# One product for both heads of a pair in each level of the RWKV inverse

## The chip, the cores and the metric

One core of a Trainium2 chip runs the whole program. The metric is the device time of one execution in microseconds, median of three runs: 1650.59 us before the change (1650.26 to 1653.68).

## The reference

Two layers of a diffusion backbone over 256 context tokens and 256 latent tokens of width 1024. Each layer mixes tokens in four parallel branches, merges them by gates, and ends in a convolutional feed-forward block. Branch D is a bidirectional RWKV-7 recurrence with four heads of 64 dimensions:

```
def step(s, inp):
    r_t, w_t, k_t, v_t, kk_t, a_t = inp
    sa = jnp.einsum('bhvk,bhk->bhv', s, kk_t)
    s = (s * w_t[:, :, None, :] - sa[..., None] * (kk_t * a_t)[:, :, None, :]
         + v_t[..., None] * k_t[:, :, None, :])
    return s, (jnp.einsum('bhvk,bhk->bhv', s, r_t) if emit else None)
```

It runs over context and then latent tokens, once forward and once backward. All is in float32.

## The kernel before

The kernel does the recurrence in eight chunks of 64 tokens. Within a chunk the effect of all `sa` terms on each other is the inverse of a 64x64 unit triangular matrix, for each head. The inverse `TN` is built by doubling: it is right for blocks of 2 tokens, and each level z of 2, 4, 8, 16, 32 joins two neighbouring blocks of z into one of 2z.

Layout: the 128 partitions hold two chunks (x = 0, 1; tokens of chunk 2b + x in half x), b runs over the four blocks of 128 tokens, p over the two pairs of heads, y over the heads of a pair. TensorE's 128x128 array is used in corners: an operand in partition half x and an output in partition half y take one 64x64 corner.

One pass is one direction of one layer, so there are four. In TensorE's program (the block of `pe`) a pass has, in this order: the masked token products (L2607, L2619), bonus and token-major copies (L2625, L2596), the five levels, u0 (L2696), `at` (L2704), the chunk recurrence (L2720 to L2736, with parts of the modulation, L2428 and L2436, between), the read-out products (L2746, L2758, L2762). A level has:

- sx (L2645), for each p: the level's triangular factor `LM1` times the even blocks of `TN`. The stationary operand is one head's 64x64 block of LM1, the moving one its 32 even columns. 16 products for each p.
- tt (L2633): `TN` of both heads turned by four 128x128 transposes for each p, copied to `TT` by ScalarE (L1322).
- jobs put between (`LEVEL_EXTRA`): LM2's products in levels 2 and 4, turned keys and `ta` in level 8, `xv` and turned betas in levels 16 and 32; in the forward passes also parts of the backward pass's preparation.
- sy (L2685), for each p: `TT` (64x64, one head and chunk) times the masked sx (`XS`), 32 columns. 16 products for each p.

VectorE masks each sx to `XS` (L1970, 256 elements a partition) and subtracts each sy from the even blocks of TN (L1987). Next level's sx waits for that subtraction. Each engine runs its program in order; the order is written by hand in one job list, and results go to PSUM banks that are handed out in that order. Weights of 1 MB stream through a ring of three slots by SP's queue; ScalarE and VectorE split them into high and low parts (L1065, L1610).

Of the kernel before, what the change touches and what calls it, by code (L numbers as in the profile page):

```python
# [74 lines left out]
for _n, _c in VEC_COLS:  # L75
# [7 lines left out]
              ("m2", CH2), ("m4", CH2), ("m8", CH2), ("m16", CH2), ("m32", CH2), ("eye", CH), ("cos", LAT), ("sin", LAT),  # L83
# [31 lines left out]
def constants():  # L115
# [303 lines left out]
def build(nc, a, out):  # L419
    ctx = ExitStack()  # L420
    with ctx:
# [283 lines left out]
        def even_blocks(v, z):  # L705

            if len(v.shape) == 2:
                return v.rearrange("p (g two n) -> p g two n", two=2, n=z)[:, :, 0, :]
            return v.rearrange("p b y (g two n) -> p b y g two n", two=2, n=z)[:, :, :, :, 0, :]
# [883 lines left out]
        def _(dve):  # L1593
# [136 lines left out]
            for l in range(LAYERS):  # L1730
# [205 lines left out]
                for d in range(2):  # L1936
                    it = 2 * l + d

                    def masked(name, LM, p):
                        h = slice(2 * p, 2 * p + 2)  # L1940
                        s = filled(dve, (name, l, d, p)).rearrange("p y (b n) -> p y b n", b=NB)
                        if l:
                            dve.tensor_tensor(LM[:, h, 0:2, 0:CH], s[:, :, 0:2, 0:CH],
                                              K("lm", CH).unsqueeze(1).unsqueeze(1).to_broadcast([P, 2, 2, CH]), ALU.mult)
                        b0 = 2 * l
                        dve.tensor_tensor(LM[:, h, b0:, :], s[:, :, b0:, :],
                                          K("lm", 2 * CH).unsqueeze(1).unsqueeze(1).to_broadcast([P, 2, NB - b0, 2 * CH]),
                                          ALU.mult).then_inc(frees((name, l, d, p)), 1)

                    def half_mask(name):  # L1950
                        return K(name, CH2).unsqueeze(1).unsqueeze(1).to_broadcast([P, 2, NB, CH2])
# [338 lines left out]
        def _(pe):  # L2290
# [201 lines left out]
            for l in range(LAYERS):  # L2492
# [97 lines left out]
                for d in range(2):  # L2590
# [7 lines left out]

                    def corners():
# [36 lines left out]
                    for n, z in enumerate(LEVELS):  # L2636
                        for p in range(2):
# [13 lines left out]
                        for extra in LEVEL_EXTRA(l, d, n):  # L2651
# [19 lines left out]
                            elif extra[0] == "xv":  # L2671
# [3 lines left out]
                                for b, x, y in corners():  # L2675
                                    h = 2 * p + y
                                    last = pe.matmul(o[side(y), x, CH * b:CH * b + CH], LM2[side(x), h, b, 0:CH],
                                                     tokm["v"][side(x), b, HD * h:HD * h + HD], start=True, stop=True)
                                done(last)
                        for p in range(2):  # L2680
# [69 lines left out]
                    for p in range(2):  # L2750
                        o = job(("y23", l, d, p))
                        for c in range(NCH // 2 * l, NCH):
# [3 lines left out]
                            for y in range(2):  # L2756
                                h = 2 * p + y
                                pe.matmul(o[side(y), x, dst], tokm["v"][side(x), b, HD * h:HD * h + HD],  # L2758
                                          LM2[side(x), h, b, CH:2 * CH], start=True, stop=False)
                            for y in range(2):  # L2760
                                h = 2 * p + y
# [140 lines left out]
```

## Time and profile before

| | |
|---|---|
| median of three runs | 1650.59 us |
| profiled execution | 1652.26 us, its span 1650.2 us |
| TensorE matmul, busy | 1586.6 us, 96% |
| TensorE weight loads, busy | 1321.7 us, 80% |
| VectorE / ScalarE / GpSimd, busy | 944.0 / 799.6 / 312.5 us |
| mean granted TensorE clock | 0.990 |

### The profile page before, as it was taken

The page shows a single profiled execution, that of the slowest core. Times are in us where ns is not written, and L with a number is a line of the kernel's source. Part 1 is how long each engine was busy: PE and PEld are TensorE (multiplying, and loading weights), DVE is VectorE, ACT ScalarE, POOL GpSimd, SP SyncE. Part 2 cuts the span into 40 slices and gives each one's busy share as a digit, 9 for nine tenths or more (in the row PEclk, how much of TensorE's full clock was granted, in tenths as well). Part 3 has the DMA queues.
Part 4 walks back from the last instruction along what each step waited for, and adds up shares of the span by engine and source line. Part 5 has one row for each costly group of instructions (what it writes and reads, how often), then busy time and mean ns, then how long its engine had stood idle before and what let it go on. Part 6 is the DMA issues. An engine that isn't in the chain of part 4 may idle for free.

```text
span 1650.2 us, 33271 instructions
## 1 busy us (share of the span) xinstructions
PE 1586.6 (96%) x14140; PEld 1321.7 (80%) x14140; DVE 944.0 (57%) x1497; ACT 799.6 (48%) x1315; POOL 312.5 (19%) x251
## 2 busy tenths in 40 slices
PE   8999999988899999999999999999998889999998
PEld 6788767767678887888888886987877779899987
DVE  5364555565465569655554225655776277677764
ACT  4322456473354266443443225525766365566653
POOL 0160234323110000112222000312352220012210
PEclk9999999999999999999999999999999899999999
DMA  9753334223852352322226343843413285645453
GB/s 332 198 166 102 102 103 160 75 99 102 266 192 91 113 191 77 102 91 88 95 71 111 106 123 126 261 128 115 143 56 130 55 281 179 215 165 181 164 189 134
DMA packets 213889, 234.42 MB, mean 142 GB/s; under 512 B 5936, under 2 KB 194736, under 8 KB 213744
## 3 DMA queue, kind: packets, MB, share of 16 engines
q1 hardware_dynamic: 194208, 191.14, 35.3%
q0 software_dynamic: 14928, 34.87, 7.9%
q10 hardware_dynamic: 4608, 6.29, 1.1%
q8 instruction: 114, 1.87, 0.5%
q14 instruction: 31, 0.25, 0.0%
HBM read 216.55 MB, written 15.73 MB: 141 GB/s over the span
## 4 chain that ended last, share of the span: by engine, by line
PE 70%; DVE 4%; issue 3%; ACT 3%; DMA 0%; POOL 0%; ACTq 0%; DVEq 0%; POOLq 0%
PE ps L2337 15%; PE ps L2338 15%; PE ps L2339 15%; PE ps L2633 1%; PE ps L2645 1%; PE ps L2428 1%; PE ps L2794 1%; PE ps L2793 1%; PE ps L2792 1%; PE ps L2685 1%; PE ps L2402 1%; PE ps L2404 1%; PE ps L2403 1%; PE ps L2362 1%; PE ps L2363 1%
## 5 line engine op out<-in xcount | busy, mean ns | idle before, releaser
L1065 ACT ACTIVATE whi<-ring 128x1024 fp32r<-128x1024 f32 (+1 forms) x262 | 274.5, 1052 | 481.6 <-PE ps L2339 424.6
L1610 DVE TENSOR_TENSOR wlo<-ring,whi 128x1024 fp32r<-128x1024 f32 (+1 forms) x262 | 327.5, 1254 | 175.5 <-ACT whi L1065 174.8
L2337 PE MATMUL ps<-H,whi 128*128 128x256 f32 (+1 forms) x640 | 215.4, 337 | 1.8 <-DVE wlo L1610 1.8
L2339 PE MATMUL ps<-H,wlo 128*128 128x256 f32 (+1 forms) x640 | 214.9, 336 | 0.0
L2338 PE MATMUL ps<-H,whi 128*128 128x256 f32 (+1 forms) x640 | 214.9, 336 | 0.0
L2337 PE MATMUL ps<-HR,whi 128*128 128x512 f32 (+1 forms) x568 | 202.1, 356 | 0.5 <-DVE wlo L1610 0.3
L2339 PE MATMUL ps<-HR,wlo 128*128 128x512 f32 (+1 forms) x568 | 198.3, 349 | 0.0
L2338 PE MATMUL ps<-HR,whi 128*128 128x512 f32 (+1 forms) x568 | 198.2, 349 | 0.0
L2337 PEld LDWEIGHTS ps<-H,whi 128*128 128x128 f32 x640 | 122.3, 191 | 14.2 <-issue 1.9
L2338 PEld LDWEIGHTS ps<-H,whi 128*128 128x128 f32 x640 | 122.2, 191 | 12.2
L2339 PEld LDWEIGHTS ps<-H,wlo 128*128 128x128 f32 x640 | 122.3, 191 | 12.0
L2337 PEld LDWEIGHTS ps<-HR,whi 128*128 128x128 f32 x568 | 107.5, 189 | 18.1 <-issue 3.8
L2338 PEld LDWEIGHTS ps<-HR,whi 128*128 128x128 f32 x568 | 107.5, 189 | 14.0 <-issue 0.7
L2339 PEld LDWEIGHTS ps<-HR,wlo 128*128 128x128 f32 x568 | 107.4, 189 | 14.1
L956 POOL TENSOR_SCALAR pr<-pr,stat 128x512 f32<-128x512 f32 (+1 forms) x48 | 72.3, 1517 | 233.2 <-DVE stat L1908 233.2
L2337 PE MATMUL ps<-HG,whi 128*128 128x512 f32 (+1 forms) x256 | 87.5, 342 | 1.5 <-DVE YB L2051 1.0
L1021 POOL TENSOR_TENSOR CU<-CU,rs 128x512 f32<-128x512 f32 (+1 forms) x22 | 40.1, 1825 | 256.2 <-ACT rs L1547 256.2
L2339 PE MATMUL ps<-HG,wlo 128*128 128x512 f32 (+1 forms) x256 | 86.5, 338 | 0.0
L2338 PE MATMUL ps<-HG,whi 128*128 128x512 f32 (+1 forms) x256 | 86.5, 338 | 0.0
L1021 POOL TENSOR_TENSOR CU<-CU,rt 128x512 f32<-128x512 f32 (+1 forms) x22 | 39.7, 1804 | 139.0 <-ACT rt L1547 139.0
L2337 PE MATMUL ps<-UA,whi 128*128 128x512 f32 x160 | 62.2, 389 | 0.0
L2338 PE MATMUL ps<-UA,whi 128*128 128x512 f32 x160 | 62.2, 389 | 0.0
(397 smaller groups left out, 3279.9 us busy)
## 6 DMA issues: line engine op xcount, KB each, us to landing
ring<-in_ffn_up SPq DMA_DIRECT2D x44, 1024.0 KB, 5.0
ring<-in_w_gate SPq DMA_DIRECT2D x32, 1024.0 KB, 5.9
ring<-in_ada_w SPq DMA_DIRECT2D x32, 1024.0 KB, 5.3
ring<-in_w_in SPq DMA_DIRECT2D x24, 1024.0 KB, 7.6
ring<-in_ffn_down SPq DMA_DIRECT2D x10, 1024.0 KB, 5.0
ring<-in_ffn_down SPq DMA_DIRECT2D x18, 512.0 KB, 3.8
ada<-in_ada_w SPq DMA_DIRECT2D x8, 1024.0 KB, 11.7
WB<-in_w_branch POOLq DMA_DIRECT2D x8, 1024.0 KB, 6.5
```

Of the source, the lines that this page charges most:

```text
L956: pool.tensor_scalar(pr[:, u % 4, 0:nk], pr[:, u % 4, 0:nk], stat[:, 2, u % 4:u % 4 + 1], None, ALU.mult).then_inc(p_ready, 1)
L1021: pool.tensor_tensor(u, u, (rs, rt)[j % 2][:, c0:c1], ALU.mult).then_inc(u_ready, 1)
L1065: act.activation(whi[HALF_SLOT[m]][:, 0:kn, :], ring_half(raw, half, kn), ACT.Copy).then_inc(hi_done, 1)
L1610: dve.tensor_tensor(wlo[HALF_SLOT[m]][:, 0:kn, :], ring_half(raw, half, kn), whi[HALF_SLOT[m]][:, 0:kn, :].bitcast(F32), ALU.subtract).the ...
L2337: pe.matmul(o[:, c0:c1], hi[:, i, :], part(0, k), start=(k == 0), stop=False)
L2338: pe.matmul(o[:, c0:c1], hi[:, i, :], part(1, k), start=False, stop=False)
L2339: last = pe.matmul(o[:, c0:c1], lo[:, i, :], part(0, k), start=False, stop=(k == kn - 1))
L2362: pe.matmul(o, hi[:, k, :], part(0, k)[:, c0:c1], start=(k == 0), stop=False)
L2363: pe.matmul(o, hi[:, k, :], part(1, k)[:, c0:c1], start=False, stop=False)
L2402: pe.matmul(outs[b], u[0], wide(hi, x), start=(k == 0), stop=False)
L2403: pe.matmul(outs[b], u[0], wide(lo, x), start=False, stop=False)
L2404: last = pe.matmul(outs[b], u[1], wide(hi, x), start=False, stop=(k == FT - 1))
```

## The change

In each level both heads of a pair share one product.

- sx: the stationary operand is both heads' blocks of LM1 (64 rows, 128 columns), the moving one the even blocks of both heads' TN (64 columns). The output has 128 partitions and 64 columns for each chunk; where one head meets the other it holds values that nobody wants. 8 products for each p.
- The masks m2 to m32 are 64 wide and also zero those mixed blocks. `XS` doubles to 512 elements a partition.
- sy: the stationary operand is TT with all 128 rows (64 columns), the moving one XS with 128 rows and 64 columns; a zeroed half adds nothing. 8 products for each p, in one bank.
- LM1 and LM2 are laid out with the two heads side by side. The constants grow by 160 columns.

```diff
-              ("m2", CH2), ("m4", CH2), ("m8", CH2), ("m16", CH2), ("m32", CH2), ...
+              ("m2", CH), ("m4", CH), ("m8", CH), ("m16", CH), ("m32", CH), ...
@@ constants
-        put(f"m{z}", ((s // z) % 2 == 1) & (even // z == s // z - 1))
+        own = ((s // z) % 2 == 1) & (even // z == s // z - 1)
+        put(f"m{z}", np.concatenate([own & (p[:, None] // CH == y) for y in range(2)], 1))
@@ buffers
-        XS = at("XS", 88, [2, 2, NB, CH2])
+        XS = at("XS", 88, [2, 2, NB, 2 * CH2])
-        LM1 = at("LM1", 96, [HEADS, NB, 2 * CH])
-        LM2 = at("LM2", 104, [HEADS, NB, 2 * CH])
+        LM1 = at("LM1", 96, [2, NB, 2, 2, CH])
+        LM2 = at("LM2", 104, [2, NB, 2, 2, CH])
@@ VectorE, masked() (the same element counts, written p b a y n)
-                        s = filled(dve, (name, l, d, p)).rearrange("p y (b n) -> p y b n", b=NB)
+                        s = filled(dve, (name, l, d, p)).rearrange("p y (b a n) -> p y b a n", b=NB, a=2)
+                        o = LM[:, p, :, :, :, :].rearrange("p b a y n -> p y b a n")
@@ VectorE, each level
-                            s = filled(dve, ("sx", l, d, z, p))[:, :, 0:NB * CH2].rearrange("p x (b n) -> p x b n", b=NB)
-                            dve.tensor_tensor(XS[:, p, :, :, :], s, half_mask(f"m{z}"), ALU.mult)\
+                            s = filled(dve, ("sx", l, d, z, p))[:, :, 0:NB * CH].rearrange("p x (b n) -> p x b n", b=NB)
+                            dve.tensor_tensor(XS[:, p, :, :, :], s, own_head(f"m{z}"), ALU.mult)\
...
-                            s = filled(dve, ("sy", l, d, z, p))[:, :, 0:NB * CH2]                                .rearrange("p y (b g n) -> p b y g n", b=NB, n=z)
-                            t = even_blocks(TN[:, p, :, :, :], z)
+                            s = filled(dve, ("sy", l, d, z, p))[:, 0, 0:NB * CH].rearrange("p (g n) -> p g n", n=z)
+                            t = even_blocks(TN[:, p, :, :, :].rearrange("p b y n -> p (b y n)"), z)
@@ TensorE, sx
-                            for b, x, y in corners():
-                                last = pe.matmul(o[side(y), x, CH2 * b:CH2 * b + CH2].rearrange("k (g n) -> k g n", n=z),
-                                                 LM1[side(x), 2 * p + y, b, 0:CH], even_blocks(TN[side(x), p, b, y, :], z),
+                            for b, x in chunks:
+                                both = TN[side(x), p, b, :, :].rearrange("p y n -> p (y n)")
+                                last = pe.matmul(o[:, x, CH * b:CH * b + CH].rearrange("k (g n) -> k g n", n=z),
+                                                 LM1[side(x), p, b, 0, :, :].rearrange("k y n -> k (y n)"), even_blocks(both, z),
@@ TensorE, sy
-                            for b, x, y in corners():
-                                last = pe.matmul(o[side(x), y, CH2 * b:CH2 * b + CH2], TT[side(y), p, b, x, :],
-                                                 XS[side(y), p, x, b, :], start=True, stop=True)
+                            for b, x in chunks:
+                                last = pe.matmul(o[side(x), 0, CH * b:CH * b + CH], TT[:, p, b, x, :],
+                                                 XS[:, p, x, b, :], start=True, stop=True)
```

## Rows read from the trace of the kernel before

**Rows 1.** The page: engines' busy time; the chain that ended last, by engine.
```profile
PE 1586.6 (96%) x14140; PEld 1321.7 (80%) x14140; DVE 944.0 (57%) x1497; ACT 799.6 (48%) x1315; POOL 312.5 (19%) x251
PE 70%; DVE 4%; issue 3%; ACT 3%; DMA 0%; POOL 0%; ACTq 0%; DVEq 0%; POOLq 0%
```

**Rows 2.** Table of stretches: a backward pass's levels, first layer.
```profile
core 0: us, PE busy (x) PEld busy (x) DVE busy (x) ACT busy (x) POOL busy (x), PEclk, DMA share, GB/s
388.00:417.40 29.40, 25.45 (x898) 22.73 (x896) 10.68 (x23) 12.64 (x24) 9.42 (x11) 1.00 0.39 111
```

**Rows 3.** Groups by form: shapes, count, busy us, mean ns, idle before.
```profile
L2645 PEld LDWEIGHTS ps<-TN,LM 64*64 64x64 f32 x1280 | 22.6, 134 | 12.6 <-issue 11.3 <-DVE TN L1987 1.2
...
L2436 PEld LDWEIGHTS ps<-con,mrow 128*128 128x128 f32 x192 | 25.0, 190 | 9.4 <-issue 7.4
...
L2540 PEld LDWEIGHTS ps<-lora,w2a 64*128 64x128 f32 x32 | 2.4, 184 | 2.1 <-issue 2.1
...
L1970 DVE TENSOR_TENSOR XS<-ps,con 128x256 f32<-128x256 f32 x40 | 16.6, 423 | 13.5 <-PE ps L2645 13.2
...
L1963 DVE TENSOR_TENSOR TN<-ps,con 128x512 f32<-128x512 f32 x8 | 5.4, 680 | 0.0
```

**Rows 4.** Timeline (start us, us, engine, line), products in levels 2 and 4.
```profile
322.92 1.10 PE L2607 MATMUL ps<-ar,zk 64*64 64x128 f32 x32
323.85 1.08 PE L2685 MATMUL ps<-XS,TT 64*64 64x32 f32 x64
...
327.47 1.09 PE L2633 MATMUL ps<-con,TN 128*128 128x128 f32 x8
328.50 1.10 PE L2607 MATMUL ps<-ar,zk 64*64 64x128 f32 x32
...
393.00 1.14 PE L2645 MATMUL ps<-TN,LM 64*64 64x32 f32 x64 [0.82 <-issue]
```

**Rows 5.** Timeline, weight loads of four forms, each from its own stretch.
```profile
427.00 0.52 PEld L2436 LDWEIGHTS ps<-con,mrow 128*128 128x128 f32 x4
...
329.53 0.30 PEld L2540 LDWEIGHTS ps<-lora,w2a 64*128 64x128 f32 x4 [0.17 <-issue]
...
334.94 1.94 PEld L2664 LDWEIGHTS ps<-con,ar 64*64 64x64 f32 x63 [0.17 <-issue]
...
313.03 0.88 PEld L2585 LDWEIGHTS ps<-prT,E 128*64 128x64 f32 x16 [1.04 <-issue]
```

**Rows 6.** DMA issues: the later part of the constants.
```profile
con<-in_const SPq DMA_DIRECT2D x1, 944.0 KB, 11.2
```

**Rows 7.** Timeline, loads of the second pair's sx in level 2.
```profile
321.27 0.59 PEld L2645 LDWEIGHTS ps<-TN,LM 64*64 64x64 f32 x32 [0.39 <-issue]
...
1279.54 0.59 PEld L2645 LDWEIGHTS ps<-TN,LM 64*64 64x64 f32 x32 [0.69 <-issue]
```

**Rows 8.** Timeline, where TensorE resumes; idle time before in brackets.
```profile
414.01 0.20 PEld L2677 LDWEIGHTS ps<-X,LM 64*64 64x64 f32 x4 [1.43 <-issue]
...
1291.54 0.86 PEld L2633 LDWEIGHTS ps<-con,TN 128*128 128x128 f32 x8 [1.80 <-issue]
...
1304.85 0.29 PEld L2645 LDWEIGHTS ps<-TN,LM 64*64 64x64 f32 x4 [2.38 <-issue]
...
446.80 0.27 PE L2762 MATMUL ps<-LM,nu 64*64 64x64 f32 x2 [2.79 <-issue]
```

**Rows 9.** The page: DMA queue of TensorE's instructions; packets, MB, share.
```profile
q8 instruction: 114, 1.87, 0.5%
```

**Rows 10.** Timeline and stretch (PEclk third from last), last level to u0, backward passes.
```profile
411.01 0.86 PEld L2633 LDWEIGHTS ps<-con,TN 128*128 128x128 f32 x8
417.41 0.79 PEld L2696 LDWEIGHTS ps<-XV,TT 64*64 64x64 f32 x43 [0.46 <-ACT TT L1322]
...
1305.21 1.57 PEld L2633 LDWEIGHTS ps<-con,TN 128*128 128x128 f32 x8
1312.97 1.76 PEld L2696 LDWEIGHTS ps<-XV,TT 64*64 64x64 f32 x64 [0.33 <-ACT TT L1322]
...
1305.00:1313.00 8.00, 8.00 (x125) 6.76 (x124) 1.41 (x4) 2.99 (x5) 2.15 (x3) 0.50 0.28 68
```

More of the change, by code:

```diff
@@ L82 @@
 CONST_COLS = [("ones", P), ("fold", 2), ("ident", P), ("heads", P), ("swap", P), ("lm", 2 * CH), ("m1", CH),
-              ("m2", CH2), ("m4", CH2), ("m8", CH2), ("m16", CH2), ("m32", CH2), ("eye", CH), ("cos", LAT), ("sin", LAT),
+              ("m2", CH), ("m4", CH), ("m8", CH), ("m16", CH), ("m32", CH), ("eye", CH), ("cos", LAT), ("sin", LAT),
               ("reset", T), ("window", GRID_W)]
@@ L705, in even_blocks @@
         def even_blocks(v, z):
-            if len(v.shape) == 2:
-                return v.rearrange("p (g two n) -> p g two n", two=2, n=z)[:, :, 0, :]
-            return v.rearrange("p b y (g two n) -> p b y g two n", two=2, n=z)[:, :, :, :, 0, :]
+            return v.rearrange("p (g two n) -> p g two n", two=2, n=z)[:, :, 0, :]
         def done_at(name):
@@ L1939, in masked, with own_head @@
                     def masked(name, LM, p):
-                        h = slice(2 * p, 2 * p + 2)
-                        s = filled(dve, (name, l, d, p)).rearrange("p y (b n) -> p y b n", b=NB)
+                        s = filled(dve, (name, l, d, p)).rearrange("p y (b a n) -> p y b a n", b=NB, a=2)
+                        o = LM[:, p, :, :, :, :].rearrange("p b a y n -> p y b a n")
                         if l:
-                            dve.tensor_tensor(LM[:, h, 0:2, 0:CH], s[:, :, 0:2, 0:CH],
+                            dve.tensor_tensor(o[:, :, 0:2, 0, :], s[:, :, 0:2, 0, :],
                                               K("lm", CH).unsqueeze(1).unsqueeze(1).to_broadcast([P, 2, 2, CH]), ALU.mult)
                         b0 = 2 * l
-                        dve.tensor_tensor(LM[:, h, b0:, :], s[:, :, b0:, :],
-                                          K("lm", 2 * CH).unsqueeze(1).unsqueeze(1).to_broadcast([P, 2, NB - b0, 2 * CH]),
+                        mask = K("lm", 2 * CH).rearrange("p (a n) -> p a n", a=2)
+                        dve.tensor_tensor(o[:, :, b0:, :, :], s[:, :, b0:, :, :],
+                                          mask.unsqueeze(1).unsqueeze(1).to_broadcast([P, 2, NB - b0, 2, CH]),
                                           ALU.mult).then_inc(frees((name, l, d, p)), 1)
-                    def half_mask(name):
-                        return K(name, CH2).unsqueeze(1).unsqueeze(1).to_broadcast([P, 2, NB, CH2])
+                    def own_head(name):
+                        return K(name, CH).unsqueeze(1).unsqueeze(1).to_broadcast([P, 2, NB, CH])
                     def square_mask(name):
@@ L2597, in token_major @@
                         done(last)
+                    chunks = [(c // 2, c % 2) for c in range(NCH)]
                     def corners():
@@ L2676, in _ @@
                                     h = 2 * p + y
-                                    last = pe.matmul(o[side(y), x, CH * b:CH * b + CH], LM2[side(x), h, b, 0:CH],
+                                    last = pe.matmul(o[side(y), x, CH * b:CH * b + CH], LM2[side(x), p, b, 0, y, :],
                                                      tokm["v"][side(x), b, HD * h:HD * h + HD], start=True, stop=True)
@@ L2758, in _ @@
                                 pe.matmul(o[side(y), x, dst], tokm["v"][side(x), b, HD * h:HD * h + HD],
-                                          LM2[side(x), h, b, CH:2 * CH], start=True, stop=False)
+                                          LM2[side(x), p, b, 1, y, :], start=True, stop=False)
                             for y in range(2):
-                                h = 2 * p + y
                                 last = pe.matmul(o[side(y), x, dst], nu[side(x), b, y, HD * p:HD * p + HD],
-                                                 LM1[side(x), h, b, CH:2 * CH], start=False, stop=True)
+                                                 LM1[side(x), p, b, 1, y, :], start=False, stop=True)
                         done(last)
```

## The prediction

> **What bounds the kernel now.** I read the page first: TensorE is busy for 96% of the span and carries most of the chain of waits [rows 1]. So time added to TensorE's stream is added to the kernel, unless TensorE was waiting there. The change lies in the RWKV inverse: four passes (two layers, two directions) of five levels, 20 levels of a first product (sx), four-block transposes (tt), other small jobs, and a second product (sy). The table of stretches gives one such pass 29.4 us, with 898 matmul records and 896 weight loads in it [rows 2]. All four together are some 128 us.
>
> In the groups by form, what a level issues is 64 records for sx and 64 for sy. An fp32 product is two records, and 1280 records over 20 levels is 64 each [rows 3]. Yet 64 records take only 1.14 us on the timeline [rows 4], though one lasts 0.22: four 64x64 corners of the array run side by side.
>
> What times them is the load of the stationary operand. 64 loads take 1.05 us, the last of them 0.135 [rows 3], so the other 0.91 us are 15 steps of about 0.06 us for four loads at once. Two corners alone, with a moving operand of 64 columns instead of 32, keep the same step: 63 loads in 1.94 us, 31 steps, 0.058 us (the third of [rows 5]). So neither moving columns up to 64 nor the number of corners counts here, but the 64 stationary columns do.
>
> **First product.** Its 64 records become 32: two row halves side by side, 128 stationary columns, 64 moving. Two rows show loads of 128 columns. Where the moving operand is 2 wide, so that only the load can take time, four take 0.52 us, the last 0.19: 0.11 us a step (the first of [rows 5]; its mean of 190 ns in [rows 3]). In the 64*128 form, four take 0.30 us with a mean of 0.184: one further step of 0.115 us for a pair, so the halves load side by side (the second of [rows 5]; its mean in [rows 3]). New loads: 16 steps, 15 x 0.11 + 0.19 = 1.84 us; the products end about 0.1 us behind, as now (1.14 against 1.05). That is some 1.98 us against 1.14, **+0.84 us a level, +16.8 us in 20**. Bounds: 0 if a step stayed at 0.058, and +50 us if the halves loaded one after another (32 steps of 0.11, 3.6 us). I take 0.11, as both rows of 128 columns have it.
>
> **Second product.** 64 records become 32 in the 128*64 form, two column halves, 64 stationary columns, 64 moving. The same form with 128 moving columns loads 16 in 0.88 us, 0.106 us a pair (the fourth of [rows 5]); two 64*64 corners with 64 moving columns need 0.058. The load has 64 columns and the moving operand has 64, so the second is nearer: 16 steps of 0.058, as now. **0**; upper bound 16 x 0.048 = 0.77 a level, +15 us; lower bound 0, since the load's own step stays.
>
> **Changes of shape.** Between products of one shape the next begins before the last ends: sy starts at 323.85 behind LM2's products that end at 324.02 (322.92 + 1.10), 0.17 us early. Behind a change of shape it is 0.06 early (327.47 + 1.09 = 328.56, next at 328.50) [rows 4]. New changes come where the job ahead of sy is 64*64: levels 2 and 8 of the forward direction, levels 2, 4 and 8 of the backward one, 10 in all. Each costs 0.11 us; sy to sx changes shape too, but there TensorE waits for VectorE anyway. **+1.2 us** with the first load in the open; 0 to 2.
>
> **VectorE.** The mask of sx goes from 256 to 512 elements a partition, 0.42 to about 0.68 us (the row of a 512-element masked copy) [rows 3], 40 times, +10 us of VectorE time. Its cover is tt and the jobs between sx and sy, over 2 us in every level; without it 0.26 us a level would show at most, 5 us. It also sits ahead of the LM2 masks in the queue, but those wait for products issued behind tt. The subtraction stays at 256 elements. The other layout of LM1 and LM2 leaves element counts as they are, so 0. The constants grow by 80 KB on 944 [rows 6], in the weights' queue at the start: 80 of 1024 KB, by the 11.2 us to landing at most 0.9, I take **+0.1 us**.
>
> **What goes: waits.** In the first level the second pair's sx waits for VectorE's first inverse in three of the passes: 0.39 and 0.69 us [rows 7], and 0.16 between them in time. The first pair's sx now takes 0.42 us longer and covers that: 0.39 + 0.42 + 0.16, **-1.0 us**.
>
> The larger item: TensorE stops in the midst of a stream of equal products, with nothing before it but "issue", most in the backward passes: 1.43, 1.80 and 2.38 us are the longest [rows 8]. I count ten such stops in the levels, with a sum of 9.0 us (the others are 0.46, 0.79, 0.44, 0.68, 0.56, 0.16 and 0.25). The page's queue of instructions gives a reason: 114 packets, 1.87 MB, 16.4 KB each [rows 9]. TensorE's 28280 loads and matmuls over 114 packets make 248 a packet. Counting loads, products and waits in the order of the trace, the stops lie 256 instructions or a multiple apart. In the backward pass 1794 instructions in 29.4 us are a packet every 4.2 us [rows 2]; over the whole kernel it is one in 14.5. The change takes 640 instructions out of a pass, and stretches it: 1154 in about 31 us, one packet in 6.9 us. I expect all ten stops to go, **-9.0 us** (0 to -9).
>
> The Trainium skill ("Runtime: NRT & Kernel Launch", "Instruction fetch mechanics") has the same 16 KiB blocks of 256 instructions, but says their fetch is hidden by the pace of issue. By that rule the stops have another cause and stay; that is rival 2.
>
> Behind the stop of 2.38 us the granted clock is 0.50, the lower level (1.2 GHz), for the rest of that pass. From the transposes of its last level to u0 it takes 1305.21 to 1312.97, 7.76 us; the same stretch of the other backward pass at full clock takes 411.01 to 417.41, 6.40, less its stop of 1.5, 4.9 us [rows 8, 10]. The difference is 2.9 us. If the stop goes, what precedes the fall of the clock goes: **-2.9 us** (0 to -3.5, with u0 in it).
>
> **Sum.** 16.8 + 0 + 1.2 + 0.1 - 1.0 - 9.0 - 2.9 = **+5.2 us**. On the profiled execution (1652.26 us, span 1650.2) that is 1657.5. It stands 1.7 us above the median of 1650.59, and stops and clock differ from run to run, so I put the change on the median: **1655.8 us**.
>
> **Rivals.**
> 1. *The wide load costs no more than the narrow one in a stream* (0.058 a pair). Place: sx in all 20 levels. Then the sum is 5.2 - 16.8 = -11.6, **1639.0**: faster. Each 0.01 us on the step is 16 x 20 x 0.01 = 3.2 us, so it turns from slower to faster below 0.094 us. For it: no row has a long stream of 64*128. Against it: both rows of 128 columns, one of them with nothing else to time it.
> 2. *The stops stay*, being the loads of saved activations that POOL issues then, or slow fetches whatever the pace. No -9.0 and no -2.9: +17.1, **1667.7**. For it: the backward passes have those DMAs. Against it: the spacing by 256 instructions.
> 3. *The relief reaches further.* The same stops come behind the passes, 2.79 us in the read-out products of the first layer's backward pass (the last of [rows 8]) and one like it in the forward pass. Fewer instructions shift where packets end there: one of the two and one of 1.6 us in u0 gone makes 5.2 - 4.3 = +0.9, **1651.5**: the same. Against it: these bursts keep all their instructions.
> 4. *Column halves of sy don't run in step*: 0.106 a pair, +15, **1670.8**. The Trainium skill ("TensorE: Matmul & The Clock Gate", "Part 3: Packing small matmuls") says that a load overlaps running products only where the row group differs; with all 128 rows in use it would not here. The 128*64 row speaks against the worst of it: 16 loads with 128-column products would take over twice its 0.88 us if nothing ran side by side.
>
> That the change does not do what it says I give no weight: the diff halves both loops over corners.
>
> **Chances.** Forecast 0.45 (own range 1651.5 to 1660: 0.10 of it same, 0.35 slower); rival 1: 0.12; rival 2: 0.15; rival 3: 0.20 (0.12 same, 0.08 faster); rival 4: 0.08. Within 0.2% (3.3 us) is about what a measurement can't tell from no change. Faster 0.20, same 0.22, slower 0.58. The range for 8 in 10 reaches to rival 1 and rival 2: 1641 to 1669.
>
> **What would show it.** In the profile after: 640 records each for sx and sy; the 32 loads of a level's sx in about 1.84 us, those of sy in 1.05; no "issue" idle over 0.4 us within the levels of the backward passes; 104 packets in the instruction queue (2560 instructions less, 10 packets); clock 1.00 to the end of the last pass. It is wrong if sx's step is not 0.11, if sy takes over 1.2 us, or if stops of 1 us and more are still there with half as many records.

## The result, and the profile after

| | before | after |
|---|---|---|
| median, first comparison (7 runs each) | 1652.69 us | 1663.24 us |
| its spread | 1650.26 to 1654.57 | 1656.89 to 1672.27 |
| ratio, 95% interval | | 1.0072 [1.0045, 1.0098] |
| profiled execution, its span | 1652.26, 1650.2 | 1672.27, 1670.3 |

The change made the kernel slower, by some 10.5 us here and by 12.8 in a second comparison (below). 1655.8 was forecast, +5.2; slower had 0.58, and the time is in the range. By the number alone rival 2 (1667.7) is nearer than the forecast; only the traces tell the two apart. The profiled execution after is the slowest of its seven, so the 20 us between the two profiles are not the change's price; much of this part is about taking them apart.

The page of the kernel after: engines' busy time and TensorE's instruction queue, which answer to [rows 1, 9].

```profile
PE 1611.6 (96%) x12860; PEld 1341.4 (80%) x12860; DVE 955.0 (57%) x1497; ACT 799.2 (48%) x1315; POOL 313.6 (19%) x251
...
q8 instruction: 104, 1.70, 0.4%
```

The groups by form of the kernel after, for [rows 3]: shapes, count, busy us, mean ns, idle before.

```profile
L2648 PE MATMUL ps<-TN,LM 64*128 64x64 f32 x640 | 40.6, 274 | 6.1 <-issue 3.9 <-DVE TN L1987 1.1 <-DVE LM L1946 0.2
L2648 PEld LDWEIGHTS ps<-TN,LM 64*128 64x128 f32 x640 | 38.1, 187 | 8.8 <-issue 6.9 <-DVE TN L1987 1.7
L1970 DVE TENSOR_TENSOR XS<-ps,con 128x512 f32<-128x512 f32 x40 | 27.7, 692 | 15.1 <-PE ps L2648 14.8
L2688 PE MATMUL ps<-XS,TT 128*64 128x64 f32 x640 | 23.0, 225 | 0.0
L2688 PEld LDWEIGHTS ps<-XS,TT 128*64 128x64 f32 x640 | 20.3, 138 | 6.5 <-issue 4.7 <-ACT X L1306 1.5
L1987 DVE TENSOR_TENSOR TN<-TN,ps 128x256 f32<-128x256 f32 x40 | 16.2, 419 | 32.5 <-PE ps L2688 31.9
```

TensorE has 1280 matmuls and 1280 loads less, and 25 us more busy time, 10 of them in one stretch at 1.2 GHz (below). The loads of sx are half as many and take 38.1 us instead of 22.6; those of sy are half as many and take 20.3 instead of the 22.6 of this row of the kernel before:

```profile
L2685 PEld LDWEIGHTS ps<-XS,TT 64*64 64x64 f32 x1280 | 22.6, 139 | 7.0 <-issue 4.6 <-ACT X L1307 2.3
```

In VectorE only the mask has grown, 423 to 692 ns.

The timeline of the kernel after, one level of the first pass, then loads of sx and sy, for [rows 4]; the last line is from the read-out products behind the first layer's backward pass, for the last of [rows 8].

```profile
322.94 1.10 PE L2609 MATMUL ps<-ar,zk 64*64 64x128 f32 x32
323.97 1.15 PE L2688 MATMUL ps<-XS,TT 128*64 128x64 f32 x32
326.42 2.00 PE L2648 MATMUL ps<-TN,LM 64*128 64x64 f32 x32 [1.30 <-issue]
328.35 1.09 PE L2635 MATMUL ps<-con,TN 128*128 128x128 f32 x8
...
326.39 1.89 PEld L2648 LDWEIGHTS ps<-TN,LM 64*128 64x128 f32 x32 [1.41 <-issue]
...
331.47 1.01 PEld L2688 LDWEIGHTS ps<-XS,TT 128*64 128x64 f32 x32 [0.76 <-issue]
...
449.14 0.27 PE L2764 MATMUL ps<-LM,nu 64*64 64x64 f32 x2 [3.33 <-issue]
```

Here the forecast's two main readings can be checked: 32 loads of sx in 1.89 us (1.84 forecast), 32 of sy in 1.01 (1.05). The long stop in the read-out products did not go with the others; it is 3.33 us now.

The table of stretches of the kernel after: the levels of both backward passes (the first for [rows 2]), the last chunk recurrence, and two stretches behind it. PEclk is the third number from the end.

```profile
390.10:421.00 30.90, 29.14 (x581) 26.22 (x580) 14.21 (x24) 12.55 (x24) 9.40 (x11) 1.00 0.36 101
...
1285.00:1315.20 30.20, 28.83 (x577) 25.81 (x576) 13.93 (x27) 12.45 (x24) 7.99 (x11) 1.00 0.23 55
1320.90:1348.20 27.30, 26.81 (x332) 18.99 (x334) 9.08 (x28) 4.75 (x8) 0.00 (x0) 0.50 0.65 203
1348.97:1358.38 9.41, 6.49 (x51) 6.04 (x50) 5.25 (x12) 4.57 (x10) 2.35 (x3) 1.00 0.83 256
1358.40:1365.20 6.80, 4.36 (x20) 4.39 (x21) 5.05 (x8) 6.11 (x9) 3.40 (x5) 0.50 0.77 263
```

The levels of a pass are timed on the timeline from the first record of sx to the first of u0. All four, in the two profiles (us; the sums are of unrounded times):

| | forward 1 | backward 1 | forward 2 | backward 2 | sum |
|---|---|---|---|---|---|
| before | 32.1 | 29.3 | 31.2 | 34.7 | 127.3 |
| after | 35.4 | 30.9 | 35.0 | 30.2 | 131.4 |

So the levels make 4 of the 20 us. The last chunk recurrence is the next part: from the start of its first product to the start of its last it took 14.7 us before and 24.8 after, at 1.2 GHz. The rest is behind the read-out products: TensorE waits 5.4 us for the first transfer of the branch weights, from 1355.5 to 1360.8, across the last two stretches of the table, and within that wait the clock falls, for 6.8 us.

### The profile page after: what moved, and what is told of

Its sections match the earlier page's. It is cut to its first block and busy times, and to the rows that moved or that the text cites. A ratio compares the mean times of both kernels' runs of the same rounds, so it can differ in the third digit from the quotient of the medians.

```text
span 1670.3 us, 30711 instructions
## 1 busy us (share of the span) xinstructions
PE 1611.6 (96%) x12860; PEld 1341.4 (80%) x12860; DVE 955.0 (57%) x1497; ACT 799.2 (48%) x1315; POOL 313.6 (19%) x251
## 5 line engine op out<-in xcount | busy, mean ns | idle before, releaser
L2243 DVE SCALAR_TENSOR_TENSOR CU<-ps,vec,CU 128x510 f32<-128x510 f32 (+1 forms) x44 | 27.1, 616 | 62.4 <-ACT CU L1541 62.4
L2337 PE MATMUL ps<-UA,whi 128*128 128x512 f32 x160 | 62.2, 389 | 0.0
## 6 DMA issues: line engine op xcount, KB each, us to landing
ada<-in_ada_w SPq DMA_DIRECT2D x8, 1024.0 KB, 11.9
```

The lines of the kernel that those rows point to most:

```text
L2243: link(dve.scalar_tensor_tensor(o[:, :, 1:256], s[:, :, 0:255], vc(l, "ffn_conv", 22 * g + j), o[:, :, 1:256], ALU.mult, ALU.add))
L2337: pe.matmul(o[:, c0:c1], hi[:, i, :], part(0, k), start=(k == 0), stop=False)
```

## The experiments

The theory at the start (A): the levels cost what the forecast's sum says, term by term, and the stops are late fetches of packets of instructions. Its rivals: the stops belong to GpSimd's transfers (rival 2), or the change costs something that the sum has not, outside the levels. The kernel before was run again beside each group of versions, with a median of 1649.89, 1650.76, 1650.75 and 1650.92 us (15, 29, 29 and 18 runs).

**after_again**: the changed kernel once more.

> The changed kernel unedited, beside the others, to see its runs with their clocks. If the clock is what lies between the fastest and the slowest run, span and mean clock go together: about 0.4 us of span for each us at half clock, the fastest near before + 4 us. If something else (contention of weights' DMA) makes the spread, runs of one clock differ by more than 4 us.

Measured 1662.64 us (10 runs), ratio 1.0073 [1.0047, 1.0099]; the medians are 12.8 us apart. In this profile a recurrence of the first pass, too, ran at 1.2 GHz. In 17 runs of the changed kernel the mean granted clock was 0.989, in the 15 of before 0.990. So the falls of the clock differ from run to run in both, and they make little of the difference of the medians. A line through the times of each kernel's runs over their mean clocks (17 runs of the changed kernel, 91 of before) gives 1663.1 and 1651.4 us at a clock of 0.990: 11.7 us apart at an equal clock. By the same line a thousandth of the mean clock goes with 1.2 us in the changed kernel. Both are estimates from these runs.

**sx_only**: only the first product is shared.

```diff
-                            for b, x in chunks:
-                                last = pe.matmul(o[side(x), 0, CH * b:CH * b + CH], TT[:, p, b, x, :],
-                                                 XS[:, p, x, b, :], start=True, stop=True)
+                            for b, x, y in corners():
+                                last = pe.matmul(o[side(x), y, CH2 * b:CH2 * b + CH2], TT[side(y), p, b, x, :],
+                                                 XS[side(y), p, x, b, CH2 * y:CH2 * y + CH2], start=True, stop=True)
```

> Only the first product is shared (64*128 form); the second stays in 64x64 corners, the mask over 512 elements stays. Theory A: 20 x 0.82 us for the loads, 1.0 us covered, no new changes of shape, all or nearly all 9 us of stops gone since a packet lasts 5 us and more: +6 us on before at equal granted clock, about 1658 to 1660. Theory B: stops stay, +15 us, about 1668. If the extra of the full change over its own sum comes from the clock in the recurrence, this kernel shows it too: runs spread over 10 us, the slow ones with the lower mean clock.

Measured 1672.03 us (6 runs), 1.0121 [1.0087, 1.0154]: too slow for the expectation. Its sx takes 1.73 us from first start to last in 17 of 20 levels, as in the changed kernel (0.92 in before). Its runs had a mean clock of 0.984, but the one at 0.990 took 1662.37, 11 us over before where +6 was expected, so the clock is not all of it. In its profile TensorE waits 4.17 us for the first branch weights, as in the changed kernel, and a recurrence ran at 1.2 GHz. Why it stands 9 us over the whole change was not settled. The load term holds; the median doesn't measure it cleanly.

**wide_twice**: sx keeps the wide load and goes corner by corner again, so that each wide load comes twice.

```diff
-                            for b, x in chunks:
-                                both = TN[side(x), p, b, :, :].rearrange("p y n -> p (y n)")
-                                last = pe.matmul(o[:, x, CH * b:CH * b + CH].rearrange("k (g n) -> k g n", n=z),
+                            for b, x, y in corners():
+                                both = TN[side(x), p, b, y, :]
+                                last = pe.matmul(o[:, x, CH * b + CH2 * y:CH * b + CH2 * y + CH2].rearrange("k (g n) -> k g n", n=z),
```

> The changed kernel with the number of wide loads doubled: the first product keeps its 128-column stationary operand (both heads' blocks of LM1) but goes corner by corner again, 64 records a level, each with one head's 32 moving columns. Same output, same masks, same second product. If the load of 128 stationary columns sets the pace (my step of 0.11 us for two halves side by side), a level's first product has 32 steps: 3.4 to 3.5 us from first to last start instead of 1.73, +1.7 to +1.76 us a level, +35 us in 20 levels, and 1280 instructions more bring back some of the stops (0 to 5 us): 1698 to 1703 us. Rival: the 64 moving columns set the pace (the products, not the loads). Then half the columns for each product keep a level's time at about 1.75 to 2.0 us, and the time is 1663 to 1670 us.

Measured 1722.76 us (5 runs), 1.0434 [1.0409, 1.0459]. Its loads of sx by form:

```profile
L2648 PEld LDWEIGHTS ps<-TN,LM 64*128 64x128 f32 x1280 | 78.3, 197 | 9.7 <-issue 7.9 <-DVE TN L1987 1.7
```

Two levels of its timeline, one usual and one across a fall of the clock:

```profile
337.64 3.69 PEld L2648 LDWEIGHTS ps<-TN,LM 64*128 64x128 f32 x64 [0.36 <-issue]
...
1247.83 5.51 PEld L2648 LDWEIGHTS ps<-TN,LM 64*128 64x128 f32 x64 [1.33 <-issue]
```

The second of them up to the fall of the clock and behind it, and the stretches of the four passes' levels:

```profile
1247.83:1249.40 1.57, 1.56 (x28) 1.57 (x29) 1.00 (x2) 0.00 (x0) 0.27 (x1) 1.00 0.07 21
1249.40:1253.40 4.00, 4.00 (x40) 3.95 (x38) 0.69 (x1) 0.00 (x0) 0.00 (x0) 0.50 0.00 0
...
319.70:370.00 50.30, 47.98 (x749) 41.73 (x748) 21.73 (x35) 25.64 (x42) 5.13 (x5) 0.86 0.01 2
406.30:450.60 44.30, 42.53 (x740) 39.19 (x739) 13.36 (x23) 13.11 (x24) 9.26 (x11) 0.88 0.23 69
1247.80:1299.10 51.30, 49.29 (x750) 42.02 (x751) 21.75 (x38) 23.85 (x40) 3.22 (x4) 0.83 0.01 3
1329.30:1375.40 46.10, 45.00 (x740) 41.23 (x740) 14.45 (x27) 12.21 (x23) 7.11 (x10) 0.81 0.15 36
```

First to last start is 3.50 us in most levels, twice the 1.73: the wide load sets the pace at 0.11 us for two halves, and the number of moving columns does not, since it was halved here. Its total is 20 us over the expectation, and the clock is the only cause that its profile shows. The 5.51 us hold no stop (a row of the timeline ends at an idle time of 0.15 us): up to 1249.4 two halves load in 0.11 us, behind it, at 1.2 GHz, in 0.21. In all, 14, 11, 17 and 18 us of the four stretches were at 1.2 GHz (twice the share that PEclk lacks), up to 30 us of delay if all of it waited for TensorE. The stops that the expectation allowed for (0 to 5 us) are not there: none is left in the midst of equal products in its levels, where 256 instructions now last 7.7 us (1474 in the 44.3 us of the second stretch of levels).

**hg_late**: rival 2. GpSimd's eight transfers of saved activations (4 MB) go out behind `at`, so that the levels have none beside them.

```diff
-GATE_INPUT_BEHIND = [("tok", "k", 1), ("sx", 16, 1), ("tt", 16, 1), ("sy", 16, 1),
-                     ("sx", 32, 1), ("tt", 32, 1), ("sy", 32, 1), ("u0", 1)]
+GATE_INPUT_BEHIND = [("at", 1)] * 8
```

> The kernel before, with the eight loads of saved activations (4 MB and 2 MB) moved behind the last product ahead of the chunk recurrence, so that none runs beside the levels. Theory A: stops at the same places, every 256 instructions, a little shorter (their packets meet no other DMA), 5 us or more of 9 left; total within 3 us of before. Theory B: the stops in the levels of the backward passes go, 6 to 9 us faster than before.

Measured 1671.53 us (6 runs), 1.0125 [1.0092, 1.0157]: both expectations missed. The 4 MB are now beside the modulation weights of the recurrence, and TensorE waits for these; it also waits 4.7 us for the first branch weights, and the mean clock of its runs is 0.980. In its table of waits (us in total, times, longest) the recurrence of the first layer's backward pass has this line:

```profile
PE ps L2427 <- DMA ring<-in_ada_w: 8.0, 1, 8.0
```

On its timeline, the stops in the last pass's levels, and the last work of GpSimd in them, which is no transfer:

```profile
1289.50 0.59 PEld L2644 LDWEIGHTS ps<-TN,LM 64*64 64x64 f32 x32 [0.69 <-issue]
1293.27 0.37 PEld L2684 LDWEIGHTS ps<-XS,TT 64*64 64x64 f32 x18 [0.67 <-issue]
1300.94 0.86 PEld L2632 LDWEIGHTS ps<-con,TN 128*128 128x128 f32 x8 [1.50 <-issue]
...
1290.78 0.73 POOL L949 TENSOR_TENSOR bm<-bm,ksc 128x256 f32<-128x256 f32 x1
```

The time says nothing about the stops, the trace does: without a transfer beside them the stops are still there, at the same count of instructions modulo 256 as in before, somewhat shorter (1.50 the longest, against 2.38 in [rows 8]). That refutes rival 2 as their cause. The transfers may lengthen them.

What releases TensorE can be read from the trace's records of the instruction queue itself, which the page only sums up (q8). In before, packets of 16384 bytes have come in at 412.69, 1289.86 and 1303.43 us; TensorE resumes from its three longest stops at 414.01, 1291.42 and 1304.85, 1.32, 1.56 and 1.42 us later. The same holds for every stop of 0.2 us and more in the midst of a pair's equal products: in the levels of before, hg_late, before_wb and before_ones each one ends 1.2 to 1.6 us behind the end of a packet. Where TensorE waits for VectorE, between the two pairs' sx, there is no such distance (anything up to 4.3 us). So the stops are waits for instructions.

**sy_shared**: only the second product is shared; VectorE masks sx once into each head's columns.

```diff
-                            dve.tensor_tensor(XS[:, p, :, :, :], s, own_head(f"m{z}"), ALU.mult)\
+                            for y in range(2):
+                                m = K(f"m{z}", CH)[:, CH2 * y:CH2 * y + CH2].unsqueeze(1).unsqueeze(1)
+                                last = dve.tensor_tensor(XS[:, p, :, :, CH2 * y:CH2 * y + CH2], s,
+                                                         m.to_broadcast([P, 2, NB, CH2]), ALU.mult)
+                            last\
@@ TensorE, sx: the loop over corners() of the kernel before
```

> Only the second product is shared. The first product is as before: 64 records of 64x64 corners with 32 moving columns, loads of 64 stationary columns. VectorE masks it twice, once into each head's columns (two operations of 256 elements a partition, 0.42 us each by the row of before, against one of 0.69 in the shared version), so that XS has zeros in the mixed blocks; the second product is the shared one. By my sum: the term of +16.8 us (wide loads) is gone, the shape changes stay (+1.2), 1280 TensorE instructions less than before, so perhaps half of the 9.0 us of stops at instruction-packet boundaries goes. Theory A: 1650 + 1.2 - 4.5 = 1646 to 1648 us, first product's 64 records in 1.0 us between the first start and the last, second product's 32 in 0.93. Theory B, by the run in which only the first product was shared (1672.03, 8.8 us over the full change): sharing the second product by itself gives back 8 to 9 us, 1641 to 1642 us. Theory C (the second mask operation delays the second product, for want of cover): 0.16 us x 20 more, 1650 to 1652 us.

Measured 1656.22 us (12 runs, 1646.77 to 1675.73), 1.0037 [1.0012, 1.0063], the ratio without the slowest run: all three expectations missed. Its levels take 31.5, 26.9, 30.5 and 28.5 us, 117.5 in all, 7 to 10 less than in the profiles of before and before_wb: with narrow loads and 109 packets the levels do get faster. Yet the kernel doesn't. Its mean clock was 0.982; by lines as above it is 2 us under before at an equal clock of 0.990, the near end of what theory A asked for. Its profile has this recurrence, in the first layer's backward pass (table of stretches):

```profile
420.00:450.60 30.60, 30.60 (x351) 21.53 (x355) 9.85 (x29) 5.13 (x9) 0.00 (x0) 0.51 0.71 225
```

The same recurrence of the kernel before:

```profile
425.00:441.10 16.10, 15.46 (x273) 10.99 (x275) 6.69 (x24) 2.31 (x6) 0.00 (x0) 1.00 0.89 306
```

And the timeline of sy_shared just ahead of its fall, with two waits:

```profile
417.75 0.74 PE L2710 MATMUL ps<-TT,X 64*64 64x64 f32 x18 [1.40 <-issue]
...
419.99 0.45 PE L2726 MATMUL ps<-state,AT 64*64 64x64 f32 x8 [0.97 <-ACT AT L1369]
```

In the profiles so far and in the two that follow (after_wb and sy_shared_wb) eight recurrences run at 1.2 GHz from their start, for 20 us or more. In all eight the fall comes within 0.7 us of the recurrence's first `cu` product, which stands behind a wait of 0.6 to 1.2 us for `AT` or for the state. (hg_late's comes in the wait for weights.) But all the other recurrences of the ten profiles have such a wait too and don't fall there, so the wait is not enough by itself. Two theories: the fall follows from the idle time at the start (K1), or from what the recurrence itself runs, small products one after another (K2). Both are tested below.

**before_wb and after_wb**: in the profile of before TensorE waits 1.57 us for the first branch weights, in that of after 5.37 (3.11 in that of after_again). GpSimd's and SP's transfers there, before and then after:

```profile
1335.44 0.93 POOL L995 DMA_DIRECT2D WB<-in_w_branch  x1 [18.49 <-PE ps L2762]
...
1337.15 0.37 SPq L838 DMA_DIRECT2D ring<-in_w_gate  x1
...
1344.53 0.36 PE L2792 MATMUL ps<-YH,WH 128*128 128x256 f32 x1 [1.57 <-DVE WL L2087]
```
```profile
1348.97 0.92 POOL L994 DMA_DIRECT2D WB<-in_w_branch  x1 [28.94 <-PE ps L2764]
...
1349.42 0.37 SPq L837 DMA_DIRECT2D ring<-in_w_gate  x1
...
1360.84 0.55 PE L2794 MATMUL ps<-YH,WH 128*128 128x256 f32 x1 [5.37 <-DVE WL L2087]
```

Before, SP's transfer of 1 MB begins 1.7 us behind GpSimd's. GpSimd's own next transfer into WB, which waits for the first, goes out 6.3 us behind it (1341.75). After, SP's begins 0.45 us behind GpSimd's, and the next goes out after 9.8 us (1358.81). Both kernels, with GpSimd's transfer sent behind y1:

```diff
-                pool.wait_ge(mm_done, done_at(("y23", l, 1, 1)))
+                pool.wait_ge(mm_done, done_at(("y1", l, 1, 1)))
@@ behind the transfer into WB
+                    if J == 0:
+                        pool.wait_ge(mm_done, done_at(("y23", l, 1, 1)))
```

> The kernel before, with one wait of GpSimd moved: the first transfer of the branch weights (1 MB into WB) goes out behind the first read-out products (y1) instead of behind the last ones (y23), about 2 us earlier; the gate transfers that were behind it still wait for y23. In the profile of before TensorE waits 1.6 us for these weights in the second layer, in that of the changed kernel 5.4 us: there the ring's transfer of 1 MB by SP went out 0.5 us before GpSimd's was under way, in before it went out 1.7 us behind it. Theory A (this race is part of what the change costs): before gains little, 0 to 2 us, 1648 to 1650 us. Rival (the branch weights' wait is paid elsewhere): no difference, 1650 us, in this one and in its partner.

> The changed kernel with the same wait moved as in its partner. Its levels cost some 6 to 7 us over before at full clock by the profile; at equal mean clock the runs differ by 9 to 12 us, so 3 to 5 us are made elsewhere. Theory A: they are the later branch weights; with them sent 2 us earlier the changed kernel gains 2 to 5 us, 1658 to 1661 us, and stands 7 to 9 us over its partner instead of 11 to 13. Rival theory R: the rest is the chunk recurrence at half clock (24.8 us instead of 14.6 in the profiled run); then this changes nothing, 1663 us, and the distance to the partner stays 12 to 13 us.

(J == 0 is the first of the transfers into WB.) Measured 1650.35 us, 0.9999 [0.998, 1.0017], and 1658.58 us, 1.0047 [1.003, 1.0063] (12 runs each). Before gains nothing, after 4 us, as theory A has it, and the pair is 8.2 us apart. The wait in after_wb's profile:

```profile
1346.65 0.92 POOL L994 DMA_DIRECT2D WB<-in_w_branch  x1 [17.72 <-PE ps L2751]
...
1348.51 0.37 SPq L837 DMA_DIRECT2D ring<-in_w_gate  x1
...
1357.03 0.36 PE L2796 MATMUL ps<-YH,WH 128*128 128x256 f32 x1 [1.57 <-DVE WL L2089]
```

SP's transfer is 1.9 us behind again, and TensorE waits 1.57 us. Over all profiles the two go together: where SP's transfer is 0.45 to 0.7 us behind (after, after_again, sx_only, hg_late) TensorE waits 3.1 to 5.4 us, in the ten others, with 1.7 to 2.6 us, at most 1.6. So the longer wait is shown. Its price in the median is not: the intervals of after_again and after_wb overlap a little, and after_wb's runs had the higher mean clock, 0.993 against 0.989. By lines as above only 1.3 of the 4 us are left at an equal clock. Some of the clock may belong to the wait, since in after the fall of 6.8 us begins within it, and in after_wb none comes with it; how much was not settled.

**sy_shared_wb, warm_start, warm_chunks**: the second product shared, with the moved wait; then with products of ones where TensorE waits for `AT` (warm_start: 5 and 0 in the line with the count), and in each chunk too (warm_chunks, as shown).

```diff
+                            o = job(("cu", l, d, c))
+                            for _ in range(5 if c == 1 else 1):
+                                pe.matmul(o[:, 0, 0:P], K("ones"), K("ones"), start=True, stop=True)
                             if c == 1:
                                 for p in range(2):
                                     emptied(pe, ("at", l, d, p))
                             emptied(pe, ("ch", l, d, c - 1))
-                            o = job(("cu", l, d, c))
```

> The version that shares only the second product, with the first branch-weights transfer sent behind y1 instead of y23. sy_shared ran 1656.22 us at a mean granted clock of 0.982 over its runs, where the kernel before has 0.990; its profile has 30.7 us at half clock in the chunk recurrence of the first layer's backward pass, and its fastest run, at 0.991, took 1646.77. If that loss of clock comes by chance and not with the version, it is gone here or smaller, and with the wait moved it takes 1646 to 1650 us. If sharing the second product brings it (fewer or shorter records before the recurrence), the clock stays at 0.98 to 0.985 and the time at 1653 to 1657 us.

> sy_shared_wb with five products of 128x128 ones (0.21 us each at full clock), written to a bank that is overwritten behind them, at the start of each chunk recurrence, where TensorE waits 0.9 to 1.2 us for ScalarE's copy of AT. Their cost is 0 to 0.3 us in each of four passes. Theory K1 (the fall of the clock in the recurrence follows from the idle time at its start): the stretches of 20 to 30 us at half clock in the recurrences go, mean clock 0.99 and over, 1643 to 1648 us. Theory K2 (it follows from what the recurrence itself runs: strips of 32 columns and 64x64 corners, one after another): nothing changes against sy_shared_wb, within 2 us.

> As warm_start, with one more such product in each of the other six chunks of every pass: 24 x 0.21 = 5 us of TensorE's time, all of it on the path if TensorE never waits there. Theory K2: the clock stays up in the recurrences (mean 0.995), which gives back 5 to 10 us where a run had the fall: 1645 to 1650 us, with a narrower spread than sy_shared_wb. Theory K1 or none: 5 us slower than warm_start.

Measured: 1655.15 us at a mean clock of 0.985, 1.0027 [1.0005, 1.0049]; 1650.60 at 0.992, 0.9993 [0.9979, 1.0008]; 1648.32 at 0.995, 0.9988 [0.9974, 1.0002] (12, 12 and 11 runs). Filling the wait at the start took 4.5 us off the median, where K2 expected no change; the intervals overlap a little. No fall begins at the start of a recurrence in the four profiles that have the filled wait (16 recurrences; 8 of 40 without it). So K1 holds for these falls. It doesn't hold alone: warm_start was to reach 1643 to 1648 us and didn't, and its profile still has a fall of 10.2 us that begins 13 us into a recurrence. And warm_chunks came out as K2 had it (1645 to 1650 us, 0.995, a narrower spread: 1644.22 to 1654.75), not 5 us over warm_start as under K1 alone: the products in the chunks, 5 us of TensorE's time by the expectation's estimate, at least pay for themselves. How the wait looks when filled (warm_start), and a recurrence of warm_chunks:

```profile
1315.97 1.38 PE L2724 MATMUL ps<-con 128*128 128x128 f32 x10
1317.28 0.45 PE L2730 MATMUL ps<-state,AT 64*64 64x64 f32 x8
```
```profile
424.80:443.00 18.20, 18.20 (x287) 13.17 (x286) 6.89 (x25) 3.42 (x8) 0.08 (x1) 1.00 0.93 298
```

That sy_shared_wb was at 0.985 again says that the low clock goes with the version. Why it falls oftener there than in before was not settled.

**before_ones and after_ones**: the change alone, with the branch weights and the clock of the recurrences held still: both kernels with the moved wait and the products of warm_chunks. The stops are not held still, since the added products shift the count of 256.

> The kernel before with both additions that keep the rest of the program the same from run to run: the earlier branch-weights transfer, and the products of ones in the chunk recurrences (5 at the start, then 1 in each chunk, up to 5 us of TensorE's time in all). It is the partner of after_ones: the pair differs only by the change. By the fits of time against clock, before_wb stood at 1647 us at a clock of 0.995; with 2 to 5 us for the products of ones 1649 to 1652 us.

> The changed kernel with the same two additions. Theory A (the levels are all that the change costs by itself: 20 x 0.81 us for the wide loads and about 1 us of changes of shape, against about 9 us of stops and 1 us of a covered wait; that is 7 to 8 us by the levels' start-to-end times in the profiles at full clock): this stands 7 to 8 us over before_ones, 1656 to 1660 us. Rival R (the change also makes the clock fall in the recurrences or delays what is behind them, 3 to 5 us on average): it stands 10 to 12 us over its partner, or, if the products of ones took that away in both, at the 7 to 8 us of theory A, but with a mean clock that is equal in the two.

Measured 1649.23 us (12 runs, 1648.02 to 1653.66), 0.9994 [0.9983, 1.0006], and 1657.03 us (7 runs), 1.0046 [1.0028, 1.0063]; the mean clock was 0.995 in both. **The pair is 7.8 us apart** (the means of the runs 8.6; drawing the runs anew at random puts that between 5.7 and 11.9). This fits theory A. It doesn't exclude the rival, which had allowed for 7 to 8 us at equal clocks with these products in; against a large share of the clock speaks that the plain kernels had about the same, 0.991 over 91 runs of before and 0.989 over 17 of the changed one.

The levels in the profiles, and how much of them was at 1.2 GHz (us):

| | sum of the levels | at 1.2 GHz |
|---|---|---|
| before, before_wb, before_ones | 127.3, 124.2, 123.7 | 8.6, 6.5, 9.5 |
| after, after_again, after_wb, after_ones | 131.4, 133.1, 131.6, 134.8 | 0, 3.4, 0, 6.8 |

The means are 125.1 and 132.7, 7.7 apart (from the unrounded sums), and no term is left out of this. Single pairs say anything from 4.1 (before, after) to 11.1 (before_ones, after_ones). The four executions of the changed kernel are each the slowest of their runs; that can make 1.3 us of the 7.7, which is what their levels have over the 131.4 of full clock.

warm_chunks is the fastest by its median, but its interval holds 1. No version is shown to beat the kernel before.

## Why the prediction was right, and where it was not

- **First product, +0.84 a level**: right. 1.73 us from first to last start against 0.92 is +0.81, 16.2 us in 20 levels. Rival 1 is out, as wide_twice shows with twice the loads.
- **Second product, 0**: right. 32 products start within 0.93 us, their loads within 0.88, in every level, though a load now uses all 128 rows. Two column halves of the array load and run side by side; rival 4 is out. That rival leaned on the rule of the Trainium skill ("TensorE: Matmul & The Clock Gate", "Part 3: Packing small matmuls") that a load overlaps running products only where the row group differs. The trace does not agree with it here: all 32 loads use all rows, and they follow each other at 0.058 us a pair while products of 0.225 us run.
- **Changes of shape, 0.11 each**: right where it can be read. sy starts 0.07 us ahead of the end of LM2's products (323.97 against 322.94 + 1.10), where it was 0.17.
- **VectorE, 0**: right. The mask grew to 692 ns, and none of the idle time ahead of sy is put down to it (6.5 us in 20 levels: issue and ScalarE's copy).
- **Covered wait, -1.0**: near. The first levels' sx are longer than 1.73 by 0.08, 0.08, 0.39 and 0.24 us, so waits of 0.8 us are left of 1.6.
- **Stops, -9.0**: the cause is right. 104 packets, as forecast, and no stop left in the midst of equal products in the levels of the changed kernel and of wide_twice (a packet in 7 us or so); sx_only and sy_shared with 109 packets keep short ones, hg_late with 114 long ones. The size is that of one execution: the stops of 1.80 and 2.38 us are 1.40 and 1.83 in before_wb, and before_ones has none over 0.5 us in its last pass. What I wrote to look for was too strict: "issue" of 0.55 to 0.75 us still stands ahead of sx in level 4 of the backward passes, but there TensorE waits for the subtraction, in both kernels. The Trainium skill ("Runtime: NRT & Kernel Launch", "Instruction fetch mechanics") calls the fetch hidden; at 4.2 us for a packet these traces show that it is not.
- **Rival 3** did not happen: the stop in the read-out products is still there, 3.33 us for 2.79.
- **Half clock in the last pass, -2.9**: the step from that one stop to the fall, and from one execution to the median, failed. In before_wb the clock falls behind stops of 1.40 and 1.43 us and holds behind the one of 1.83, which stands where before's 2.38 did; the changed kernel's levels have falls without any stop (after_again, after_ones). But that before loses time at 1.2 GHz in its levels is no single case: its two variants do too, in other passes, 6.5 and 9.5 us. So a part of this gain is there in the runs, not the whole and not by that path.
- **What the sum lacked**: the order of two transfers behind the passes. With SP's transfer nearer behind that of the first branch weights, these take 9.8 us instead of 6.3 until GpSimd goes on, and TensorE waits 1.5 to 3.8 us longer.

The sum can now be closed. For the pair of profiles before and after, the terms that hold give 16.2 + 1.2 - 0.8 = 16.6 us, the levels differ by 4.1, so 12.5 us went with stops and clock: the forecast had 11.9. It is right for the execution from which it was read. Over the seven profiles the levels differ by 7.7 us, so only 8.9 went with them. That the forecast without its clock term, 5.2 + 2.9 = 8.1, comes so near to 7.8 is partly luck: the stops were put too high and the clock would be left out altogether.

Beyond the levels 3 to 5 us are missing to the 10.5 to 12.8 that the medians show. The longer wait for the branch weights lies there and is of that order; that it is the whole was not shown. The forecast was right in direction and in the cost of the two products, and 5 to 8 us low by these two: what one execution gives back, and the transfers behind the passes.

## What to carry to other kernels

Sharing one product between two small ones halves the instructions, but a load of twice the stationary columns costs twice the time: it gains only where the instructions themselves are what is late. Widen the moving side or the rows instead, which cost nothing here (32 to 64 moving columns, 64 to 128 rows). A gain that hangs on stops or on the granted clock in one profile belongs to that execution: look for it in more profiles and in the clocks of all runs before it goes into a sum for the median. And behind a stage that changes length, look at which transfer now goes out first.

## What the runs showed of the hardware

- Loads of 64 rows by 128 columns come at 0.11 us for two row halves (0.21 at 1.2 GHz, wide_twice), of 64 by 64 at 0.058 for four corners or for two column halves with all rows, with 32 or 64 moving columns.
- TensorE stops at multiples of 256 instructions where small products run at a packet in 4 to 5 us: 0.2 to 2.4 us each, with or without transfers of GpSimd beside them. Each stop that was looked at ends 1.2 to 1.6 us behind the end of an instruction packet's transfer. At a packet in some 7 us there are none.
- In eight recurrences, each behind a wait of 0.6 to 1.2 us, a chain of small products ran at 1.2 GHz for 20 us and more: 14.7 us became 24.8. None of 16 did so from its start with five products of ones in the wait; the median of that version fell by 4.5 us.
- Wide loads with 32 moving columns (wide_twice) went with falls of the clock in all four passes: some 60 of 192 us were at 1.2 GHz. With 64 moving columns it was 0, 3.4, 0 and 6.8 of 131 to 135 us in four profiles of the changed kernel.
